# Both heads of a pair in one value group, k_lo over all 128 rows, and tiles placed at 256-byte multiples, in a decoder layer

## What is computed

```python
h = rms_norm(x, norm_mix[i])
proj = (h @ w_in[i]).astype(f32)
ya = dilated_attention(qa, ka, va, bias_a)      # softmax(q k^T * scale + bias) v, three dilations
yb = hgrn2(qb, fb, ib, gb, lb_all[i], hgrn_gnorm[i])
yc = moba_attention(qc, kc, vc, bias_c)
x = x + concat(ya, yb, yc) @ w_out[i]
u = causal_dwconv(rms_norm(x, norm_ffn[i]) @ w_up[i], conv_w[i], conv_b[i])
x = x + (silu(ug) * uv) @ w_down[i]
x = x + sigmoid(rms_norm(x, norm_ple[i]) @ w_pg[i]) * (p[i] @ w_pe[i])
return rms_norm(x, norm_final)
```

## Time and profile before

| | |
|---|---|
| median of 3 runs (lowest, highest) | 793.18 us (792.83, 793.69) |
| profiled execution: its time, the span of its instructions | 792.15 us, 790.3 us |
| TensorE busy | 770.8 us, 98% of the span |
| VectorE, ScalarE, GpSimd busy | 454.4, 315.2, 119.7 us |
| weight loads of TensorE (beside its matmuls) | 609.0 us |
| DMA, mean over the span | 88 GB/s |

### The profile page before, as it was taken

One profiled execution on the slowest core, in us unless ns is written; L12 is line 12 of the kernel. 1 busy time (PEld: TensorE's weight loads), 2 busy tenths in 40 slices (PEclk: granted clock), 3 DMA queues, 4 the chain that ended last, 5 costly groups with the idle time before them and its releaser, 6 DMA issues.

```text
span 790.3 us, 10528 instructions
## 1 busy us (share of the span) xinstructions
PE 770.8 (98%) x3935; PEld 609.0 (77%) x3935; DVE 454.4 (58%) x705; ACT 315.2 (40%) x545; POOL 119.7 (15%) x97
## 2 busy tenths in 40 slices
PE   5999999999999999999999999999999999999994
PEld 4788778867777677788888888888888888887883
DVE  4754788475545442557677676677674333333554
ACT  7652223164444443345434334334333222326344
POOL 0030000044534342121110111101110000100000
PEclk9999999999999999999999999999999999999998
DMA  8332221311211110233332333323324332334202
GB/s 248 112 105 80 59 77 54 107 53 55 80 57 51 60 47 28 66 104 99 105 106 81 106 95 91 106 86 100 106 73 127 93 92 83 98 100 134 80 1 107
DMA packets 121744, 69.43 MB, mean 88 GB/s; under 512 B 2658, under 2 KB 118450, under 8 KB 121706
## 3 DMA queue, kind: packets, MB, share of 16 engines
q1 hardware_dynamic: 119982, 65.72, 28.4%
q10 hardware_dynamic: 1724, 3.19, 1.2%
HBM read 66.77 MB, written 2.13 MB: 87 GB/s over the span
## 4 chain that ended last, share of the span: by engine, by line
PE 96%; DMA 1%; ACT 1%; DVE 1%; issue 0%; SPq 0%; ACTq 0%; DVEq 0%
PE bank L459 28%; PE bank L461 26%; PE bank L460 26%; PE bank L594 4%; PE bank L568 2%; PE bank L566 2%; PE bank L499 2%; PE bank L580 2%; DMA raw<-in_w_in 1%; PE bank L533 1%; PE bank L553 0%; PE bank L516 0%; PE bank L766 0%; ACT scratch L959 0%; PE bank L510 0%
## 5 line engine op out<-in xcount | busy, mean ns | idle before, releaser
L459 PE MATMUL bank<-h_hi,w_hi 128*128 128x512 f32 (+1 forms) x664 | 268.4, 404 | 2.7 <-DVE h_lo L1155 2.7
L461 PE MATMUL bank<-h_hi,w_lo 128*128 128x512 f32 (+1 forms) x664 | 258.2, 389 | 0.0
L460 PE MATMUL bank<-h_lo,w_hi 128*128 128x512 f32 (+1 forms) x664 | 257.6, 388 | 0.0
L822 ACT ACTIVATE w_hi<-raw 128x1024 fp32r<-128x1024 f32 (+1 forms) x116 | 120.9, 1043 | 291.1 <-PE bank L461 291.0
L1149 DVE TENSOR_TENSOR w_lo<-raw,w_hi 128x1024 fp32r<-128x1024 f32 (+1 forms) x116 | 144.6, 1247 | 115.4 <-ACT w_hi L822 115.3
L459 PEld LDWEIGHTS bank<-h_hi,w_hi 128*128 128x128 f32 x664 | 125.0, 188 | 35.0 <-issue 6.2
L461 PEld LDWEIGHTS bank<-h_hi,w_lo 128*128 128x128 f32 x664 | 125.0, 188 | 26.4
L460 PEld LDWEIGHTS bank<-h_lo,w_hi 128*128 128x128 f32 x664 | 125.3, 189 | 23.5 <-issue 1.0
L1629 POOL TENSOR_SCALAR probs<-probs,row_inv 128x512 f32<-128x512 f32 (+3 forms) x48 | 66.0, 1375 | 187.5 <-DVE row_inv L1420 187.5
L461 PE MATMUL bank<-act_hi,w_lo 128*128 128x512 f32 x176 | 70.2, 399 | 0.0
L460 PE MATMUL bank<-act_lo,w_hi 128*128 128x512 f32 x176 | 69.4, 394 | 0.0
(11 more groups left out here) (185 smaller groups left out, 812.4 us busy)
## 6 DMA issues: line engine op xcount, KB each, us to landing
raw<-in_w_up SPq DMA_DIRECT2D x44, 512.0 KB, 3.8
raw<-in_w_in SPq DMA_DIRECT2D x30, 512.0 KB, 3.9
raw<-in_w_down SPq DMA_DIRECT2D x16, 512.0 KB, 3.5
raw<-in_w_out SPq DMA_DIRECT2D x8, 512.0 KB, 3.5
raw<-in_w_pg SPq DMA_DIRECT2D x8, 512.0 KB, 3.5
bias<-bias_table ACTq DMA_DIRECT2D x6, 512.0 KB, 4.3
raw<-in_w_down SPq DMA_DIRECT2D x8, 384.0 KB, 3.2
x_rows<-in_x SPq DMA_DIRECT2D x4, 512.0 KB, 5.9
```

Source lines behind the costliest of these rows:

```text
L459: pe.matmul(bank, hi, x_hi, start=first, stop=False)
L460: pe.matmul(bank, hi, x_lo, start=False, stop=False)
L461: return pe.matmul(bank, lo, x_hi, start=False, stop=last)
L822: act.activation(w_hi[:, u % SPLIT, 0:nk * ncol], raw[:, u % RAW, 0:nk * ncol], ACT.Copy)\
```

## The change

**Order of the steps.** Step n now belongs to head 2 (n // 8) + n % 2, and its tile is 3 - (n % 8) // 2: the two heads of a pair alternate, and the keys go 512, 512, 384, 384, 256, 256, 128, 128. `values_of_both` takes the place of `step_values`. It is called on every second tick and does the value products of two steps, one of each head, with the head in the inner loop. It waits until the later step's probabilities are there, and `weighted` counts such groups, so the waits for it are rewritten.

**k_lo.** It gets a slot for each head. The head's own 64 rows hold the low part as before, the other 64 are zeros, which GpSimd writes once, at the start, with two memsets. L568 becomes a matmul over all 128 rows.

**Places.** A tile of 128 bytes stands ahead of `x_t`, `sumsq`, `scratch` and `r_row` stand ahead of the small tiles, and 160 bytes behind these. In the built program `x_t`, `h_*`, `raw`, `w_*`, `square`, and everything from `q_both` on but a few small tiles, now begin at a multiple of 256 bytes.

```diff
+def head_of(n):
+    return 2 * (n // (2 * TT)) + n % 2
 def tile_of(n):
-    return TT - 1 - n % TT
+    return TT - 1 - n % (2 * TT) // 2
...
+        sb("before_x", [P, 32])
         x_t = sb("x_t", [P, KT, SEQ])
...
+        sumsq = sb("sumsq", [P, SEQ])
+        scratch = sb("scratch", [P, 4, SEQ])
+        r_row = sb("r_row", [P, SEQ])
         vec_cols = sb("vec_cols", [P, 4 * KT + 1])
...
+        sb("after_small", [P, 40])
...
-        k_lo = sb("k_lo", [P, 3, SEQ], F32R, mixing)
+        k_lo = sb("k_lo", [P, 3, 2, SEQ], F32R, mixing)
...
+                if n == 0:
+                    pe.wait_ge(k_lo_blank, 2)
-                rows = slice(hh * HEAD, (hh + 1) * HEAD)
...
-                pe.matmul(score[n % 2][:, 0:keys], q_both[rows, pair % 3, hh, queries], k_lo[rows, pair % 3, 0:keys],
+                pe.matmul(score[n % 2][:, 0:keys], q_both[:, pair % 3, hh, queries], k_lo[:, pair % 3, hh, 0:keys],
                           start=False, stop=True).then_inc(scored, 1)
...
-            def step_values(n):
-                head, i = n // TT, tile_of(n)
-                pair, rows = head // 2, slice((head % 2) * HEAD, (head % 2 + 1) * HEAD)
-                pe.wait_ge(probs_t_ready, n + 1)
+            def values_of_both(n):
+                pair, i = n // (2 * TT), tile_of(n)
+                pe.wait_ge(probs_t_ready, n + 2)
...
                 for jb in range(i + 1):
-                    mm = pe.matmul(outs[pair % 2][rows, i * P:(i + 1) * P], v_tok[:, pair % 3, jb, rows],
-                                   probs_t[:, n % 4, jb * P:(jb + 1) * P], start=(jb == 0), stop=(jb == i))
+                    for hh in range(2):
+                        rows = slice(hh * HEAD, (hh + 1) * HEAD)
+                        mm = pe.matmul(outs[pair % 2][rows, i * P:(i + 1) * P], v_tok[:, pair % 3, jb, rows],
+                                       probs_t[:, (n + hh) % 4, jb * P:(jb + 1) * P], start=(jb == 0), stop=(jb == i))
                 mm.then_inc(weighted, 1)
 
             def tick(m):
...
-                if m >= VALUE_LAG:
-                    step_values(m - VALUE_LAG)
+                if m >= VALUE_LAG and (m - VALUE_LAG) % 2 == 1:
+                    values_of_both(m - VALUE_LAG - 1)
...
-                    act.wait_ge(weighted, n - 3)
+                    act.wait_ge(weighted, (n - 4) // 2 + 1)
...
+            for hh in range(2):
+                other = slice((1 - hh) * HEAD, (2 - hh) * HEAD)
+                if hh:
+                    pool.wait_ge(k_lo_blank, hh)
+                pool.memset(k_lo[other, :, hh, :].bitcast(F32), 0.0).then_inc(k_lo_blank, 1)
```

More of the change, by code:

```diff
@@ L556, in step_score @@
             def step_score(n):
-                head, i = n // TT, tile_of(n)
+                head, i = head_of(n), tile_of(n)
                 pair = head // 2
@@ L1422, in keep_mixed @@
             def keep_mixed(pair):
-                dve.wait_ge(weighted, 2 * TT * (pair + 1))
+                dve.wait_ge(weighted, TT * (pair + 1))
                 dve.tensor_copy(mix_a_hi[:, pair, :], outs[pair % 2][:, :]).then_inc(mix_hi_ready, 1)
```

15 lines of the change are left out of this document (6 added, 9 removed).

## The result

The changed kernel takes **751.6 us** (median of 4 runs, 750.9 to 752.16) and the kernel before, on the same chip in the same session, 793.27 us (4 runs, 792.83 to 793.69). The ratio is 0.9475, 95% interval [0.9464, 0.9486]: faster by 5.25%. The forecast was 749.0 us with the range 712 to 754. It was faster as forecast and inside the range, 2.6 us above the point. The profiled execution took 751.99 us (its span 750.2), where the sum had put it at 747.9, so 4.1 us are to be accounted for there.

A forecast was written before the change was run, and what follows sets the result against it. TensorE, holding 96% of the chain of waits, was taken to bound the kernel. The terms 18.0 + 8.0 + 13.1 + 5.1 = 44.2 us came off 793.18, giving 749.0 us, range 712 to 754.

The forecast's parts named there:

- `k_lo` over all rows: Attention's 48 low scores use the full array, so the half-row surplus goes: 18.0 us, bounds 0 and 19.8.
- fewer trips and halves in turn: Attention value products: 24 trips into half the columns instead of 48, 8.0 us; alternating column halves, 13.1 us.
- places: Moving operands of 768 matmuls no longer start at only a multiple of 32 bytes: 6.6 ns each, 5.1 us.
- memsets: GpSimd's two memsets at the start and the wait for them: nothing; without idle cover, 2 to 4 us.
- other engines: VectorE, GpSimd and ScalarE keep up with the shorter attention ticks: 0, with 1.5 us as the other end.
- no wait of TensorE for L1424 over 0.5 us: Sign to look for in the profile after: TensorE never waits longer than this for that line.
- Rival 4: Attention: VectorE's 11.06 us stretch or two wide GpSimd steps hold up scores, 1 to 4 us, 752; chance 0.04.
- The surplus of the score pair: Attention: extra time of a score pair beyond its matmuls, 0.40 us for 36 pairs, 0.30 for 12 narrow ones.
- The 13.1 us: Attention: 240 value records that alternate column halves cost 0.0546 us each instead of 0.109; other end of the bound 0.
- A start that is only a multiple of 32 bytes costs 6.6 ns: Long matmuls such as the down-projection's: moving operand 224 bytes past a multiple of 256 takes 0.2333 us, not 0.2267.
- The choice for the 1944 matmuls of `h` (nothing): Matmuls with operands 128 bytes past a multiple of 256 gain nothing from moving; bounds nothing and 25.9 us.
- the first rival: Starts at 256-byte multiples matter for all long matmuls: full gain 36.2 us more, time about 718; chance 0.28.

The follow-up runs named there:

- Head outermost: The changed kernel with the loop over the two heads outside the loop over key blocks in the value products; 756.11 us, ratio 0.953.
- the kernel at 224: The changed kernel with x, h, weights, raw and scratch 224 bytes past a multiple of 256, mixing tiles at multiples of it; 756.18 us.
- the two kernels made for it: The changed kernel with w_hi 32 and w_lo 64 bytes past a multiple of 256 (761.55 us), or with h_lo and w_hi 32 past (765.44 us).

## Why the prediction was right, and where it was off

The direction, the mechanism and each of the three places of gain were right, by the steps of the text. Term by term, the trace of before and of after, and the experiments where one part stands alone:

| term | forecast | measured |
|---|---|---|
| `k_lo` over all rows | 18.0 | 17.5 of surplus; 16.4 with the waits it brings out |
| fewer trips and halves in turn | 8.0 + 13.1 = 21.1 | 21.0 |
| places | 5.1 | 4.8 in its stages; 4.3 with the wait behind them |
| memsets | 0 | not to be told from 0 |
| other engines | 0, up to 1.5 | 1.91 at 170.9, 177.0 and 179.2 us; 0.53 at the sum of squares (counted with the places above) |
| start of unit 1 in the profiled execution | - | 0.98 later than in that of before |

**The term that failed is the last choice: "I take 0, with 1.5 as the other end".** The stretch of 11.06 us of VectorE in the earlier trace rows was the right place, and I looked for the wait there on the wrong instruction. The text reasoned by the score, which waits for the bias two ticks back, and found slack. The wait came at the value products, over ScalarE: "ScalarE's copy (L981) still has a tick between the transposes and the value products" is true, but the copy stands behind an exponential in ScalarE's order, and the exponential waits for VectorE. The second step of a pair has one tick between its transposes and its products, as every step had, but four ticks had become 2.8 us shorter (36.83 over 13 slots) and VectorE's burst had not. The forecast's own test, "no wait of TensorE for L1424 over 0.5 us", passed for this reason and told nothing: the wait is for L991. Rival 4 had the cause (VectorE's stretch of 11.06 us) and the size (1 to 4 us, 752), though it too looked for it at the scores, and got a chance of 0.04. That was far too little for a place that I had named myself.

**The surplus of the score pair** was sized from one tick at 0.40 and taken for three widths. The medians are 0.393, 0.391 and 0.384, and 0.288 for the narrow ones. This is half a microsecond.

**Alternation** was right to 0.1 us in the sum, and for the reason given, but strict alternation is more than that reason needs. The 13.1 us compare two heads in one run, alternating, with two heads in separate ticks. Head outermost keeps two thirds of it, since the two halves' chains overlap where they meet. The rule of the Trainium skill (TensorE: Matmul & The Clock Gate, Part 3), by which the 13.1 us would not have come, is not borne out: 16 records of both column halves, all over the same 128 rows, take 1.02 us to the next line, where one half alone takes that for 8.

**Places.** The number was right and the reading of it wrong, which is luck. "A start that is only a multiple of 32 bytes costs 6.6 ns" fell with the kernel at 224. The right observation stood in the same paragraph ("weights lie alike in both"), used to rule the weights out, where it meant that only the distance between the two had changed. As the change puts everything at multiples of 256, the two readings give the same sum. The choice for the 1944 matmuls of `h` (nothing) was right: 24 take 5.44 at 0, 128, 192 and 224 past. With it the first rival's 0.28 and the 0.08 for a part of it are refuted, and the low end of 712 was wider than needed.

**What I costed at nothing** besides: the memsets (nothing seen), GpSimd (no row of TensorE's waits names it in the attention stretch of the changed kernel), and the transition of the transposes to the score. The trip costs 0.35 us, as taken: from the last transpose to the fourth projection matmul behind a narrow score it is 2.251 us with a run of 16 records and 1.026 without one (medians of six ticks each in the changed kernel), less 16 x 54.6 ns. Without a run the score starts 0.03 us behind the last transpose.

**The account.** Of the 4.1 us that the profiled execution took beyond the sum, 0.98 are its later start. From unit 1 on 41.0 us came instead of 44.2, 3.2 short: 1.9 of waits in the attention, 0.5 at the sum of squares, 0.5 of surplus that wasn't there and 0.3 of the places.

## What to carry to other kernels

When two small products can use different column halves of TensorE, put them into one run and in turn (groups of up to four records of one half did nearly as well here); each run costs a trip of 0.35 us, so longer runs are better than more runs, up to the buffers they need. In the long `fp32r` matmuls here, a weight tile and the moving operand that is read while it is loaded should start alike modulo 64 bytes; when a stage is 3% slower than its twin with the same shapes, compare the addresses of both operands and not of one. And when a faster engine eats up slack, follow each in-order queue behind it for a burst: the wait shows up not on the instruction that waits for the burst's engine but on the one that is queued behind it, on a third engine.

## What was unexpected of the hardware

- A 512-wide matmul takes 6.6 ns more than its 227 when the next weights lie 32 bytes off the moving operand modulo 64; 64 bytes apart costs nothing (5.54, 5.60 and 5.57 us for 24 in the two kernels made for it, 5.44 otherwise).
- In the attention stretch this cost is nearly hidden: the same two kernels lose 0.28 and 0.25 us there, where 104 triples with 13 to 20 ns each would make 1.4 to 2.1. Projection matmuls there are 231 to 235 ns apart on average in all kernels, with the distances alike or not. What holds them up instead I have not found, and it wasn't tried.
- Records of one column half overtake those of the other, as I read the starts. A run of 8 records of the first half and then 8 of the second ran as two chains with 0.49 us between their starts, instead of one after the other.
- The start of unit 1 moved between 22.06 and 24.34 us over 14 traces with the same loads: by 1.3 us with the arrival of the second piece of `x`, and by 1.3 with the time that unit 0 spends at granted clock 0.50. A comparison from unit 1 on was ten times finer than one of whole times (727.16, 727.25 and 727.29 for three kernels that should not differ, whose medians are 751.6 to 752.98).
